# Token-row loads between the channel groups, and the third operand sum on VectorE before the second

## The chip, the cores and the metric

The kernel runs on one core of one Trainium2 chip. The metric is device time in microseconds of one execution; three runs of the kernel before are given by their median.

## The reference

A hybrid encoder layer is applied to two sequences (`x_prompt`, `x_sample`) of 1024 tokens by 1024 channels, in float32:

```
h = rmsnorm(x, norm_mix)
z = h @ w_in                      # 512 pooling, 3 x 768 attention (q, k, v)
a = pool_mixer(z[..., :512]) @ w_up_pool
b = attention_branch(z[..., 512:]) @ w_up_attn
g = sigmoid(h @ w_gate + b_gate)
x = x + (g_a * a + g_b * b) @ w_out
h = rmsnorm(x, norm_ffn)
x = x + (silu(h @ w_ffn_gate) * (h @ w_ffn_up)) @ w_ffn_down
y = rmsnorm(x, norm_final)
```

`rmsnorm` divides a token by the root of its mean square over the channels and multiplies by a gain per channel. The change touches only the first tens of microseconds: the first `rmsnorm` of the first sequence, the value columns of `h @ w_in` for two groups of heads, and the first pair of q and k columns.

## The kernel before, in words

**Precision.** Each float32 operand is split into a high part (a cast to fp32r, on ScalarE) and a low part (the rest, by a subtraction on GpSimd or VectorE). One product of two operands is three matmuls: high by high, high by low, low by high (`three`, lines 1334 to 1336).

**Products.** Most matrix products are done by a scheme with seven products instead of eight. The activations are cut into quarters: A11 and A12 are the first half of the tokens (half 0) with channels 0 to 511 and 512 to 1023, A21 and A22 those of half 1. Four sums are made of them: S1 = A21 + A22, S2 = S1 - A11, S3 = A11 - A21, S4 = A12 - S2. The products come in the order A11, S2, A12, S3, S1, A22, S4; each takes a weight operand (`t_hi`, `t_lo`) and 12 matmuls of 512 columns. The first pair of column blocks done so has the products 14 to 20; product 14 is A11, 15 is S2, 16 is A12, 17 is S3, 18 is S1.

**Opening.** Before these, the value columns of two head groups are computed directly (`direct_run`), with eight channel blocks k (128 channels each) of the transposed input, loaded as `xt` into `HT[h][p]` (half h, blocks 2p and 2p+1; a pair of blocks is called a channel group here). Run 0 takes token tiles 0 to 3 (half 0) unnormalised, four tiles by three matmuls per block; runs 1 and 2 take tiles 4, 5 and 6, 7 (half 1) normalised, six matmuls per block. The norm factors need the rows of `x` token by token (`x_rows[h][p]`, four loads per half): ScalarE squares and sums a row tile (`squares_of`), takes the root of four (`deviations`), VectorE inverts and spreads them (`factors`, tile `spread`), TensorE transposes the spread tile (`factor_rows`, put between the blocks of a direct run by the number given to it), and VectorE multiplies the channels by gain and factor (`channel_norms`). Half 1 is normalised first, then half 0. After that come casts (`open_his`, ScalarE), low parts (`open_low` on GpSimd, `open_lows` on VectorE) and sums (`open_sums` on GpSimd, `open_thirds` on VectorE).

**Order.** Every engine has its program written out by hand, in `opening` of its block; engines run their lists in order and wait on semaphores. SP issues the loads in the order of `first_tokens`, all on one queue. In the lists of ScalarE and GpSimd `operand_hi` and `leading_lows` make the high and low part of the weight operand of products 14 to 17; four more follow in the normal schedule. The buffers are placed by address: the high and low parts of S3 lie in `S` where half 1's channels lie, and the raw S2 has a buffer of its own, `s2_raw`; S3 is written over A11, S1 over A22, S4 over A12.

Of the kernel before, what the change touches and what calls it, by code (L numbers as in the profile page):

```python
# [13 lines left out]
P = 128  # L14
# [311 lines left out]
def encoder(nc, x, w_in, maps, w_up_pool, w_up_attn, w_gate, w_out, w_fg, w_fu, w_fd,  # L326
# [3 lines left out]
    with ctx:  # L330
# [35 lines left out]
        s2_raw = [at(f"s2_raw{i}", EX + 4096 * i, [2, H2]) for i in range(2)]  # L366
# [106 lines left out]
        ones_set, spread_ready, third_made, first_in, rows_in = (sem(n) for n in ("ones_set", "spread_ready", "third_made", "first_in", "rows_in"))  # L473
# [59 lines left out]
        def open_source(part, k):  # L533

            if part[0] == "A":
                ks = slice(k, k + 1)
                return channels(int(part[1] == "2"), part, ks), ks
            ks = slice(2 * k, 2 * k + 2)
            if part == "S1":
                return channels(1, "A22", ks), ks  # L540
            if part == "S2":
                return s2_raw[k][:, :, :].rearrange("q k (p c) -> q p k c", c=P), ks
            return channels(0, part, ks), ks
# [37 lines left out]
        def _(sp):  # L581
# [44 lines left out]
            def first_tokens():  # L626
# [9 lines left out]
                def rows(h, p):  # L636
                    sp.dma_start(x_rows[h][p][:, :], x_t[0, 4 * h + p]).then_inc(rows_in, 16)
# [4 lines left out]
                for p in range(4):  # L642
                    rows(1, p)
                for p in range(4):
                    sp.dma_start(HT[1][p][:, :, :], xt_k[:, 2 * p:2 * p + 2, H2:T]).then_inc(xh_in[p], 16)
                sp.wait_ge(ssx_ready, 4)
# [386 lines left out]
        def _(pool):  # L1033
# [200 lines left out]
            def open_sums(part, i):  # L1234
# [3 lines left out]
                if part == "S1":  # L1238
                    pool.wait_ge(xn_ready, XN_AT[1, 4 + 2 * i + 1])
                    for k in range(2 * i, 2 * i + 2):  # L1240
                        open_ready(pool, "A22", k)
                    out, a, b, op = s1, channels(1, "A21", ks), s1, ALU.add
                elif part == "S2":
                    pool.wait_ge(mix_made, SUMMED["S1", i])
                    out, a, b, op = s2, s1, channels(0, "A11", ks), ALU.subtract
                else:
                    pool.wait_ge(mix_made, SUMMED["S2", i])
                    for k in range(2 * i, 2 * i + 2):
                        open_ready(pool, "A12", k)
                    out, a, b, op = channels(0, "A12", ks), channels(0, "A12", ks), s2, ALU.subtract  # L1250
                nc.gpsimd.tensor_tensor(out, a, b, op).then_inc(mix_made, 1)

            def opening():
# [13 lines left out]
                leading_lows(0, 2, (0, 1))  # L1267
                for i in range(2):
                    open_sums("S4", i)
                leading_lows(0, 2, (2, 3))  # L1270
# [52 lines left out]
        def _(pe):  # L1323
# [265 lines left out]
            def warm_up():  # L1589
                pe.wait_ge(ones_set, 1)  # L1590
# [34 lines left out]
            def opening():  # L1625

                warm_up()
                direct_run(0, {5: 1})
                direct_run(1, {5: 0})
# [137 lines left out]
        def _(act):  # L1767
# [3 lines left out]
            act.wait_ge(eps_set, 1)  # L1771
# [315 lines left out]
            def squares_of(h, p):  # L2087

                act.wait_ge(rows_in, 64 if h else 128)
# [40 lines left out]
            def opening():  # L2130
# [5 lines left out]
                for p in range(4):  # L2136
                    squares_of(1, p)
                deviations(1)
# [171 lines left out]
        def _(dve):  # L2310
            nc.vector.memset(ones[:, :], 1.0).then_inc(ones_set, 1)
# [61 lines left out]
            def open_thirds():  # L2373

                for i in range(2):
                    ks = slice(2 * i, 2 * i + 2)
                    dve.wait_ge(mix_made, SUMMED["S2", i])
                    for k in range(2 * i, 2 * i + 2):
                        open_ready(dve, "A11", k)
                    a = channels(0, "A11", ks)  # L2380
                    V_.tensor_tensor(a, a, channels(1, "A21", ks), ALU.subtract).then_inc(third_made, 1)

            def opening():

# [589 lines left out]
```

## Time and profile before

| | us |
|---|---|
| three runs, median (lowest to highest) | 2507.11 (2505.29 to 2507.63) |
| the profiled execution, its own time | 2509.43 |
| its span in the profile | 2506.4 |
| TensorE busy in the span | 2477.3 (99%) |
| GpSimd busy | 1708.5 (68%) |
| VectorE busy | 1295.7 (52%) |
| ScalarE busy | 1030.9 (41%) |

The span is the time from the first to the last instruction that the profile shows; the execution's own time has some more around it. Busy shares are means over the whole span. Since TensorE is busy nearly throughout, its own pauses, and the stretches in which it is granted a lower clock, are what has to be read in detail; for the other engines the stretch around such a pause counts, not the share.

### The profile page before, as it was taken

To read this page: it belongs to the slowest core of one execution; us is meant where nothing else is said; L and a number is where in the kernel's file an instruction comes from. 1 tells how busy PE (TensorE), PEld (TensorE's weight loads), DVE (VectorE), ACT (ScalarE), POOL (GpSimd) and SP (SyncE) were. 2 spreads that over 40 slices of the span, in tenths; PEclk is the share of its full clock that TensorE was granted. 3 is DMA by queue.
4 is the path that set the end of the run, shared out by engine and by line. 5 is a ranking of instruction groups with operands and counts; after the bars stand their busy time and mean duration, and the time that the engine had idled before them with its cause. 6 is when DMAs were issued, how large, how long until landed. Compare 5 with 4: busy or idle time off the path is not lost. (4 is left out here: it accounts for less than half of the span.)

```text
span 2506.4 us, 33224 instructions
## 1 busy us (share of the span) xinstructions
PE 2477.3 (99%) x12032; PEld 2039.6 (81%) x12032; DVE 1295.7 (52%) x1740; ACT 1030.9 (41%) x1988; POOL 1708.5 (68%) x1258
## 2 busy tenths in 40 slices
PE   8999999999999999999999999999999999999998
PEld 6788877888888888888888888788888888888887
DVE  6774546645422222387956745456462222224768
ACT  6324553445433333346452245534453333333445
POOL 6865456545888888755687754573468888887544
PEclk9999999999999999999999999999999999999999
DMA  7345556462333333474353445656523332435543
GB/s 245 126 126 160 157 161 188 163 253 76 97 93 97 119 95 101 139 237 166 127 180 90 128 144 162 182 158 207 204 84 94 113 100 91 125 93 177 185 128 141
DMA packets 330272, 357.95 MB, mean 143 GB/s; under 512 B 39168, under 2 KB 234368, under 8 KB 328576
## 3 DMA queue, kind: packets, MB, share of 16 engines
q1 hardware_dynamic: 328528, 352.58, 44.2%
q10 hardware_dynamic: 1584, 3.26, 0.4%
q8 instruction: 97, 1.59, 0.3%
q14 instruction: 63, 0.52, 0.1%
HBM read 254.39 MB, written 101.38 MB: 142 GB/s over the span
## 5 line engine op out<-in xcount | busy, mean ns | idle before, releaser
L1334 PE MATMUL ps<-S,t_hi 128*128 128x512 f32 (+1 forms) x2264 | 890.3, 393 | 13.9 <-POOL t_lo L1084 11.9
L1336 PE MATMUL ps<-S,t_lo 128*128 128x512 f32 (+1 forms) x2264 | 879.7, 389 | 0.0
L1335 PE MATMUL ps<-S,t_hi 128*128 128x512 f32 (+1 forms) x2264 | 878.9, 388 | 0.0
L1334 PEld LDWEIGHTS ps<-S,t_hi 128*128 128x128 f32 x2264 | 426.1, 188 | 106.5 <-POOL t_lo L1084 14.4
L1336 PEld LDWEIGHTS ps<-S,t_lo 128*128 128x128 f32 x2264 | 425.9, 188 | 87.9
L1335 PEld LDWEIGHTS ps<-S,t_hi 128*128 128x128 f32 x2264 | 426.5, 188 | 84.7 <-issue 1.0
L1084 POOL TENSOR_TENSOR t_lo<-wraw,t_hi 128x512 fp32r<-128x512 f32 x175 | 237.3, 1357 | 186.7 <-ACT t_hi L1865 184.2
L1084 POOL TENSOR_TENSOR t_lo<-wraw_ff,t_hi 128x512 fp32r<-128x512 f32 x225 | 289.1, 1286 | 78.7 <-ACT t_hi L1865 68.6
L1084 POOL TENSOR_TENSOR t_lo<-R,t_hi 128x512 fp32r<-128x512 f32 x154 | 219.6, 1430 | 175.8 <-ACT t_hi L1865 175.6
L1865 ACT CAST t_hi<-wraw_ff 128x512 fp32r<-128x512 f32 x225 | 139.9, 623 | 364.5 <-PE ps L1336 363.2
L1334 PE MATMUL ps<-t_hi,d_hi 128*128 128x512 f32 x616 | 240.5, 390 | 0.0
L1336 PE MATMUL ps<-t_hi,d_lo 128*128 128x512 f32 x616 | 239.8, 389 | 0.0
L1335 PE MATMUL ps<-t_lo,d_hi 128*128 128x512 f32 x616 | 239.7, 389 | 0.0
L1865 ACT CAST t_hi<-wraw 128x512 fp32r<-128x512 f32 x175 | 109.2, 625 | 238.9 <-PE ps L1336 234.0
L2736 DVE TENSOR_TENSOR d_lo<-d_raw,d_hi 128x512 fp32r<-128x512 f32 x154 | 141.6, 921 | 95.8 <-ACT d_hi L2064 94.3
L2501 DVE TENSOR_TENSOR u<-u,ps 128x512 f32<-128x512 f32 x80 | 54.9, 687 | 259.3 <-PE ps L1336 259.2
L2064 ACT CAST d_hi<-d_raw 128x512 fp32r<-128x512 f32 x154 | 95.6, 621 | 173.9 <-PE ps L1336 160.7
L2504 DVE TENSOR_TENSOR v<-u,ps 128x512 f32<-128x512 f32 x80 | 55.0, 687 | 190.2 <-PE ps L1336 189.7
L1084 POOL TENSOR_TENSOR t_lo<-t,t_hi 128x512 fp32r<-128x512 f32 x70 | 94.2, 1346 | 84.5 <-ACT t_hi L1865 84.1
L1084 POOL TENSOR_TENSOR t_lo<-t_ff,t_hi 128x512 fp32r<-128x512 f32 x90 | 117.9, 1310 | 31.5 <-ACT t_hi L1865 31.5
L1216 POOL TENSOR_TENSOR wo_lo<-wo_raw,wo_hi 128x1024 fp32r<-128x1024 f32 x32 | 82.0, 2571 | 80.2 <-ACT wo_hi L2029 80.2
L1336 PEld LDWEIGHTS ps<-t_hi,d_lo 128*128 128x128 f32 x616 | 115.6, 188 | 24.4
(229 smaller groups left out, 4011.4 us busy)
## 6 DMA issues: line engine op xcount, KB each, us to landing
d_raw<-d_rows SPq DMA_DIRECT2D x154, 256.0 KB, 2.8
d_rows<-act_f SPq DMA_DIRECT2D x110, 256.0 KB, 2.2
wraw_ff<-w_ffn_up SPq DMA_DIRECT2D x44, 512.0 KB, 4.5
R<-w_ffn_down SPq DMA_DIRECT2D x88, 256.0 KB, 3.1
sp_rows<-gst SPq DMA_DIRECT2D x80, 256.0 KB, 2.2
wraw_ff<-w_ffn_gate SPq DMA_DIRECT2D x40, 512.0 KB, 5.0
wraw<-w_in SPq DMA_DIRECT2D x38, 512.0 KB, 6.0
wo_raw<-w_out SPq DMA_DIRECT2D x36, 512.0 KB, 3.7
```

Source lines behind the costliest of these rows:

```text
L1084: nc.gpsimd.tensor_tensor(shape(t_lo[r][:, :]), src, shape(t_hi[r][:, :]).bitcast(F32), ALU.subtract).then_inc(t_ready, 1)
L1216: nc.gpsimd.tensor_tensor(wo_lo[r][:, :], wo_raw[op % 3][:, :], wo_hi[r][:, :].bitcast(F32), ALU.subtract).then_inc(wo_ready, 1)
L1334: nc.tensor.matmul(o_ps, w[0], r[0], start=begins, stop=False, skip_group_check=True)
L1335: nc.tensor.matmul(o_ps, w[0], r[1], start=False, stop=False, skip_group_check=True)
L1336: return nc.tensor.matmul(o_ps, w[1], r[0], start=False, stop=ends, skip_group_check=True)
L1865: nc.scalar.copy(dst, src).then_inc(thi_ready, 1)
L2064: nc.scalar.copy(d_hi[d % 4][:, :], d_raw[d % 4][:, :]).then_inc(dhi_ready, 1)
L2501: V_.tensor_tensor(u, u, b1, ALU.add).then_inc(sums_done, 1)
L2504: V_.tensor_tensor(v1[:, :], u, b2, ALU.add).then_inc(sums_done, 1)
L2736: V_.tensor_tensor(d_lo[d % 4][:, :], d_raw[d % 4][:, :], d_hi[d % 4][:, :].bitcast(F32), ALU.subtract).then_inc(d_ready, 1)
```

## The change

**Loads.** SP issues two of half 1's four row loads behind channel group 1 and two behind group 2, ahead of groups 2 and 3; before, all four came behind group 3. ScalarE squares them between the casts of the groups, in two pairs that wait on two semaphores, and the root of half 1 comes ahead of the casts of group 3. SP releases half 0's row loads after two squares instead of four. VectorE makes half 1's factors after six of the eight raw splits. TensorE transposes half 1's factors behind block 4 of run 0 (before: block 5), and half 0's behind block 1 of run 1 (before: block 5).

**Sums.** VectorE forms S3 in a buffer of its own (where the raw S2 stood) right after the splits of A12, without waiting for S2; GpSimd writes S2 over A11 and waits for S3 first. On GpSimd the third low part of a weight operand comes ahead of the S4 sums.

```diff
-        s2_raw = [at(f"s2_raw{i}", EX + 4096 * i, [2, H2]) for i in range(2)]
+        s3_raw = [at(f"s3_raw{i}", EX + 4096 * i, [2, H2]) for i in range(2)]
...
+            if part == "S3":
+                return s3_raw[k][:, :, :].rearrange("q k (p c) -> q p k c", c=P), ks
             if part == "S2":
-                return s2_raw[k][:, :, :].rearrange("q k (p c) -> q p k c", c=P), ks
+                return channels(0, "A11", ks), ks
...
                 for p in range(4):
                     rows_of_first(p)
                     columns(p)
-                for p in range(4):
-                    rows(1, p)
+                    if p in (1, 2):
+                        rows(1, 2 * p - 2)
+                        rows(1, 2 * p - 1)
                 for p in range(4):
                     sp.dma_start(HT[1][p][:, :, :], xt_k[:, 2 * p:2 * p + 2, H2:T]).then_inc(xh_in[p], 16)
-                sp.wait_ge(ssx_ready, 4)
+                sp.wait_ge(ssx_ready, 2)
                 for p in range(4):
                     rows(0, p)
...
                 elif part == "S2":
                     pool.wait_ge(mix_made, SUMMED["S1", i])
+                    pool.wait_ge(third_made, i + 1)
+                    for k in range(2 * i, 2 * i + 2):
+                        open_ready(pool, "A11", k)
                     out, a, b, op = s2, s1, channels(0, "A11", ks), ALU.subtract
...
-                leading_lows(0, 2, (0, 1))
+                leading_lows(0, 2, (0, 1, 2))
                 for i in range(2):
                     open_sums("S4", i)
-                leading_lows(0, 2, (2, 3))
+                leading_lows(0, 2, (3,))
...
                 warm_up()
-                direct_run(0, {5: 1})
-                direct_run(1, {5: 0})
+                direct_run(0, {4: 1})
+                direct_run(1, {1: 0})
                 direct_run(2, {})
...
-                act.wait_ge(rows_in, 64 if h else 128)
+                act.wait_ge(late_rows_in if h and p > 1 else rows_in, 32 if h else 96)
...
                     elif part == "S3":
                         act.wait_ge(third_made, 2)
+                        act.wait_ge(mix_made, SUMMED["S2", 1])
...
                     raw_his(k)
-                for p in range(4):
-                    squares_of(1, p)
-                deviations(1)
+                    if k in (2, 4):
+                        squares_of(1, k - 2)
+                        squares_of(1, k - 1)
+                    if k == 4:
+                        deviations(1)
...
                     ks = slice(2 * i, 2 * i + 2)
-                    dve.wait_ge(mix_made, SUMMED["S2", i])
-                    for k in range(2 * i, 2 * i + 2):
-                        open_ready(dve, "A11", k)
-                    a = channels(0, "A11", ks)
-                    V_.tensor_tensor(a, a, channels(1, "A21", ks), ALU.subtract).then_inc(third_made, 1)
+                    a21, a11 = channels(1, "A21", ks), channels(0, "A11", ks)
+                    V_.tensor_tensor(open_source("S3", i)[0], a11, a21, ALU.subtract).then_inc(third_made, 1)
...
-                raw_lows(range(KD))
+                raw_lows(range(6))
                 factors(1)
+                raw_lows(range(6, KD))
...
-                open_lows(DVE_OPEN[8:12])
                 open_thirds()
-                open_lows(DVE_OPEN[12:])
+                open_lows(DVE_OPEN[8:])
```

The load queue of SP, from channel group 1 on, before. `ht_1_78` to `ht_3_80` are the channel groups 1 to 3 of half 0, `wraw_both` the weights that go with them, `x_rows_0_89` to `x_rows_3_92` half 1's rows:

```order
L629 DMA ht_1_78<-xt 128x2x512
L633 DMA wraw_both<-w_in 128x2x512
L629 DMA ht_2_79<-xt 128x2x512
L633 DMA wraw_both<-w_in 128x2x512
L629 DMA ht_3_80<-xt 128x2x512
L637 DMA x_rows_0_89<-x 128x1024
L637 DMA x_rows_1_90<-x 128x1024
L637 DMA x_rows_2_91<-x 128x1024
L637 DMA x_rows_3_92<-x 128x1024
```

The same place with the change:

```order
L632 DMA ht_1_78<-xt 128x2x512
L640 DMA x_rows_0_89<-x 128x1024
L640 DMA x_rows_1_90<-x 128x1024
L636 DMA wraw_both<-w_in 128x2x512
L632 DMA ht_2_79<-xt 128x2x512
L640 DMA x_rows_2_91<-x 128x1024
L640 DMA x_rows_3_92<-x 128x1024
L636 DMA wraw_both<-w_in 128x2x512
L632 DMA ht_3_80<-xt 128x2x512
```

The four row loads have moved up, two by two, ahead of groups 2 and 3; half 1's channel loads come behind these rows in both.

GpSimd from the S1 sums to the fourth weight operand, before. `ht_2_83` and `ht_3_84` become S1 there, `s_raw` is S2, `ht_2_79` and `ht_3_80` become S4; the `t_lo` rows are products 14 to 17 in order:

```order
L1251 TENSOR_TENSOR ht_2_83<-ht_0_81,ht_2_83 128x4x2x128 [waits mix_made,s_ready,xn_ready]
L1251 TENSOR_TENSOR ht_3_84<-ht_1_82,ht_3_84 128x4x2x128 [waits mix_made,s_ready,xn_ready]
L1251 TENSOR_TENSOR s_raw_116<-ht_2_83,ht_0_77 128x4x2x128 [waits mix_made]
L1251 TENSOR_TENSOR s_raw_117<-ht_3_84,ht_1_78 128x4x2x128 [waits mix_made]
L1084 TENSOR_TENSOR t_lo_137<-wraw_127,t_hi_132 128x512 [waits thi_ready]
L1084 TENSOR_TENSOR t_lo_136<-t_142,t_hi_131 128x512 [waits thi_ready]
L1251 TENSOR_TENSOR ht_2_79<-ht_2_79,s_raw_116 128x4x2x128 [waits s_ready,mix_made]
L1251 TENSOR_TENSOR ht_3_80<-ht_3_80,s_raw_117 128x4x2x128 [waits s_ready,mix_made]
L1084 TENSOR_TENSOR t_lo_138<-wraw_127,t_hi_133 128x512 [waits thi_ready]
L1084 TENSOR_TENSOR t_lo_139<-wraw_127,t_hi_134 128x512 [waits thi_ready,t_made]
```

The same place with the change, where `ht_0_77` and `ht_1_78` (A11) become S2:

```order
L1258 TENSOR_TENSOR ht_2_83<-ht_0_81,ht_2_83 128x4x2x128 [waits mix_made,s_ready,xn_ready]
L1258 TENSOR_TENSOR ht_3_84<-ht_1_82,ht_3_84 128x4x2x128 [waits mix_made,s_ready,xn_ready]
L1258 TENSOR_TENSOR ht_0_77<-ht_2_83,ht_0_77 128x4x2x128 [waits mix_made,third_made]
L1258 TENSOR_TENSOR ht_1_78<-ht_3_84,ht_1_78 128x4x2x128 [waits mix_made,third_made]
L1088 TENSOR_TENSOR t_lo_137<-wraw_127,t_hi_132 128x512 [waits thi_ready]
L1088 TENSOR_TENSOR t_lo_136<-t_142,t_hi_131 128x512 [waits thi_ready]
L1088 TENSOR_TENSOR t_lo_138<-wraw_127,t_hi_133 128x512 [waits thi_ready]
L1258 TENSOR_TENSOR ht_2_79<-ht_2_79,ht_0_77 128x4x2x128 [waits s_ready,mix_made]
L1258 TENSOR_TENSOR ht_3_80<-ht_3_80,ht_1_78 128x4x2x128 [waits s_ready,mix_made]
L1088 TENSOR_TENSOR t_lo_139<-wraw_127,t_hi_134 128x512 [waits thi_ready,t_made]
```

S2 has the new wait on `third_made`, and the `t_lo` of product 16 has moved from behind the S4 sums to ahead of them.

VectorE from the last A12 splits to the S4 splits, before. The rows with 128x4x256 are the low parts of S1 (`ht_2_83`, `ht_3_84`), S2 (`s_raw`), S3 (`ht_0_77`, `ht_1_78`) and S4 (`ht_2_79`, `ht_3_80`); the two with 128x4x2x128 are the S3 sums:

```order
L2370 TENSOR_TENSOR S<-ht_3_80,S 128x4x128 [waits shi_ready] x2
L2370 TENSOR_TENSOR S<-ht_2_83,S 128x4x256 [waits shi_ready]
L2370 TENSOR_TENSOR S<-ht_3_84,S 128x4x256 [waits shi_ready]
L2370 TENSOR_TENSOR S<-s_raw_116,S 128x4x256 [waits shi_ready]
L2370 TENSOR_TENSOR S<-s_raw_117,S 128x4x256 [waits shi_ready]
L2381 TENSOR_TENSOR ht_0_77<-ht_0_77,ht_0_81 128x4x2x128 [waits mix_made]
L2381 TENSOR_TENSOR ht_1_78<-ht_1_78,ht_1_82 128x4x2x128 [waits mix_made]
L2370 TENSOR_TENSOR S<-ht_0_77,S 128x4x256 [waits shi_ready]
L2370 TENSOR_TENSOR S<-ht_1_78,S 128x4x256 [waits shi_ready]
L2370 TENSOR_TENSOR S<-ht_2_79,S 128x4x256 [waits shi_ready]
L2370 TENSOR_TENSOR S<-ht_3_80,S 128x4x256 [waits shi_ready]
```

The same place with the change, where `s_raw` is S3 and `ht_0_77`, `ht_1_78` are S2:

```order
L2380 TENSOR_TENSOR S<-ht_3_80,S 128x4x128 [waits shi_ready] x2
L2388 TENSOR_TENSOR s_raw_116<-ht_0_77,ht_0_81 128x4x2x128
L2388 TENSOR_TENSOR s_raw_117<-ht_1_78,ht_1_82 128x4x2x128
L2380 TENSOR_TENSOR S<-ht_2_83,S 128x4x256 [waits shi_ready]
L2380 TENSOR_TENSOR S<-ht_3_84,S 128x4x256 [waits shi_ready]
L2380 TENSOR_TENSOR S<-ht_0_77,S 128x4x256 [waits shi_ready]
L2380 TENSOR_TENSOR S<-ht_1_78,S 128x4x256 [waits shi_ready]
L2380 TENSOR_TENSOR S<-s_raw_116,S 128x4x256 [waits shi_ready]
L2380 TENSOR_TENSOR S<-s_raw_117,S 128x4x256 [waits shi_ready]
L2380 TENSOR_TENSOR S<-ht_2_79,S 128x4x256 [waits shi_ready]
L2380 TENSOR_TENSOR S<-ht_3_80,S 128x4x256 [waits shi_ready]
```

The S3 sums have moved ahead of the S1 and S2 splits and have lost their wait.

## Rows read from the trace of the kernel before

**Rows 1.** The page, busy us, share of the span and instructions of each engine.
```profile
PE 2477.3 (99%) x12032; PEld 2039.6 (81%) x12032; DVE 1295.7 (52%) x1740; ACT 1030.9 (41%) x1988; POOL 1708.5 (68%) x1258
```

**Rows 2.** Waits of TensorE, 0 to 100 us: us in total, times, longest.
```profile
PE ps L1334 <- POOL t_lo L1084: 11.9, 2, 9.1
```

**Rows 3.** Stretches: length, busy us by engine, granted clock (PEclk), DMA share, GB/s.
```profile
59.40:69.70 10.30, 5.55 (x13) 4.39 (x14) 10.24 (x5) 3.34 (x6) 10.30 (x5) 0.50 0.16 52
76.50:79.90 3.40, 3.40 (x10) 2.62 (x9) 3.40 (x2) 0.18 (x1) 3.32 (x3) 0.50 0.00 0
79.90:95.00 15.10, 15.10 (x68) 12.49 (x67) 13.93 (x26) 4.56 (x8) 14.86 (x12) 1.00 0.45 140
```

**Rows 4.** Timeline of TensorE: start us, us, instruction, [idle before it <-releaser].
```profile
20.23 0.39 PE L1334 MATMUL ps<-extra_hi,raw_hi 128*128 128x512 f32 x1
...
40.80 0.63 PE L1599 MATMUL ps<-ident_sb,spread 128*128 128x128 f32 x4 [0.44 <-DVE spread L2341]
...
54.67 0.39 PE L1336 MATMUL ps<-extra_hi,S 128*128 128x512 f32 x1
...
64.15 0.79 PE L1334 MATMUL ps<-S,t_hi 128*128 128x512 f32 x1 [9.09 <-POOL t_lo L1084]
...
75.25 0.47 PE L1334 MATMUL ps<-S,t_hi 128*128 128x512 f32 x1 [2.79 <-POOL t_lo L1084]
...
82.43 0.39 PE L1334 MATMUL ps<-S,t_hi 128*128 128x512 f32 x1
```

**Rows 5.** Timeline of GpSimd from 40 us on.
```profile
43.76 5.96 POOL L1231 TENSOR_TENSOR S<-ht,S 128x512 fp32r<-128x512 f32 x4 [0.70 <-ACT S L2128]
...
55.27 6.61 POOL L1251 TENSOR_TENSOR s_raw<-ht,ht 128x1024 f32<-128x1024 f32 x2
61.85 2.25 POOL L1084 TENSOR_TENSOR t_lo<-wraw,t_hi 128x512 fp32r<-128x512 f32 x1
...
72.92 4.47 POOL L1084 TENSOR_TENSOR t_lo<-wraw,t_hi 128x512 fp32r<-128x512 f32 x2
...
79.69 2.16 POOL L1084 TENSOR_TENSOR t_lo<-t,t_hi 128x512 fp32r<-128x512 f32 x1
81.82 2.54 POOL L1084 TENSOR_TENSOR t_lo<-wraw,t_hi 128x512 fp32r<-128x512 f32 x2
```

**Rows 6.** Timeline of VectorE, 0 to 100 us.
```profile
7.79 12.34 DVE L2361 SCALAR_TENSOR_TENSOR raw_lo<-ht,gain_c,raw_hi 128x512 fp32r<-128x512 f32 x8 [6.79 <-ACT raw_hi L2084]
...
26.76 1.41 DVE L2351 SCALAR_TENSOR_TENSOR ht<-ht,gain_c,ps 128x512 f32<-128x512 f32 x2 [0.81 <-PE ps L1599]
...
41.47 4.04 DVE L2351 SCALAR_TENSOR_TENSOR ht<-ht,gain_c,ps 128x512 f32<-128x512 f32 x6 [0.81 <-PE ps L1599]
...
49.14 3.93 DVE L2370 TENSOR_TENSOR S<-ht,S 128x512 fp32r<-128x512 f32 x2
53.64 6.05 DVE L2370 TENSOR_TENSOR S<-ht,S 128x1024 fp32r<-128x1024 f32 x2 [0.57 <-ACT S L2128]
...
65.10 5.60 DVE L2381 TENSOR_TENSOR ht<-ht,ht 128x1024 f32<-128x1024 f32 x2
71.83 8.86 DVE L2370 TENSOR_TENSOR S<-ht,S 128x1024 fp32r<-128x1024 f32 x4 [1.12 <-ACT S L2128]
```

**Rows 7.** Timeline of ScalarE, 5 to 42 us.
```profile
15.37 1.34 ACT L2084 ACTIVATE raw_hi<-ht,gain_c 128x512 fp32r<-128x512 f32 x2 [0.29 <-DMA ht<-xt]
20.42 1.06 ACT L2090 ACTIVATE squares<-x_rows 128x1024 f32<-128x1024 f32 x1 [3.71 <-DMA x_rows<-x]
...
30.85 0.63 ACT L2128 CAST S<-ht 128x512 fp32r<-128x512 f32 x1 [0.64 <-DVE ht L2351]
32.94 1.06 ACT L2090 ACTIVATE squares<-x_rows 128x1024 f32<-128x1024 f32 x1 [1.46 <-DMA x_rows<-x]
```

**Rows 8.** Half 1's channel loads: issues (duration, first to last); the last, us to landing.
```profile
L645 SPq DMA_DIRECT2D ht<-xt x4: 570/1271/2329, 8.7 to 11.9; - x4
...
ht<-xt SPq DMA_DIRECT2D x1, 512.0 KB, 14.4
```

More of the change, by code:

```diff
@@ L472, in encoder @@
         upp_in = [sem(f"upp_in{r}") for r in range(2)]
-        ones_set, spread_ready, third_made, first_in, rows_in = (sem(n) for n in ("ones_set", "spread_ready", "third_made", "first_in", "rows_in"))
+        spread_ready, third_made, first_in, rows_in, late_rows_in = (sem(n) for n in (
+            "spread_ready", "third_made", "first_in", "rows_in", "late_rows_in"))
         sems = {name: sem(name) for name in PER_SEQ}
@@ L636, in rows @@
                 def rows(h, p):
-                    sp.dma_start(x_rows[h][p][:, :], x_t[0, 4 * h + p]).then_inc(rows_in, 16)
+                    sp.dma_start(x_rows[h][p][:, :], x_t[0, 4 * h + p]).then_inc(late_rows_in if h and p > 1 else rows_in, 16)
                 for p in range(4):
@@ L1589, in warm_up @@
             def warm_up():
-                pe.wait_ge(ones_set, 1)
+                pe.wait_ge(eps_set, 1)
                 for _ in range(WARM):
@@ L1770, in _ @@
                 act.dma_start(dst, src).then_inc(ident_in if src is ident else gmix_in if src is gmix else const_in, 16)
-            act.wait_ge(eps_set, 1)
+            act.wait_ge(eps_set, 2)
             nc.scalar.activation(root[:, :], eps[:, :], ACT.Sqrt)
@@ L2310, in _ @@
         def _(dve):
-            nc.vector.memset(ones[:, :], 1.0).then_inc(ones_set, 1)
+            nc.vector.memset(ones[:, :], 1.0).then_inc(eps_set, 1)
             nc.vector.memset(eps[:, :], EPS).then_inc(eps_set, 1)
```

## The prediction

> **What bounds the kernel now.** I read the page first: TensorE is busy 99% of a span of 2506.4 us [rows 1], so a change wins time only where TensorE stands still or runs slowly. The list of its waits over the first 100 us has one large entry: 11.9 us in two waits for the low halves `t_lo` that GpSimd makes [rows 2]. TensorE's timeline shows where: 9.09 us between the last direct matmul (54.67) and product 14 (64.15), and 2.79 us ahead of product 16 (75.25) [rows 4]. The stretches with their granted clock show what follows a wait: 59.4 to 69.7 and 76.5 to 79.9 ran at 0.50, which is 1.2 GHz, the rest at 2.4 GHz [rows 3]. At full clock a matmul takes 15.10/68 = 0.22 us of the engine, at half 5.55/13 = 0.43 [rows 3], 0.2 us more: 13 times 0.2 = 2.6 us behind the long wait, and half of a stretch of 3.4, 1.7 us, behind the short one. All that this opening could give back is 9.1 + 2.8 + 2.6 + 1.7 = 16 us.
>
> Who sets these waits? GpSimd has no gap worth naming from 43.76 on: A11 splits, S1 sums, S2 sums, `t_lo` of products 14 and 15, S4 sums, `t_lo` of 16 and 17, a weight sum, `t_lo` of 18 [rows 5]. Product 14 starts when its `t_lo` ends (61.85 + 2.25 = 64.10). Product 18 starts at 82.43 [rows 4] and its `t_lo` ended at 79.69 + 2.16 = 81.85 [rows 5], 0.58 us of slack. So **GpSimd's chain binds, and TensorE follows it with 0.58 us to spare**: in products 14 to 18 no more can be won than that slack plus what the chain is earlier at `t_lo` 18.
>
> The chain starts with the A11 casts, which wait for half 0's norm factors, which wait for half 0's token rows: ScalarE stood idle from the end of a cast (30.85 + 0.63) until the rows were in at 32.94, 1.46 us [rows 7].
>
> **The change part by part.**
> *Loads.* In a full queue one load of rows costs (20.42 - 15.37)/4 = 1.26 us, from the last channel group's casts to the squares that waited for the four loads behind it [rows 7]. Two rows ahead of channel group 2 make it 2.5 us later, four ahead of group 3 bring that to 15.37 + 5.05 = 20.4. Group 2 would then be in at about 15.2; its two casts take 1.34 [rows 7] and a VectorE split 12.34/8 = 1.54 [rows 6], so 18.1, and TensorE reaches channel 4 at 20.23 [rows 4]. Two microseconds cover it; group 3 is needed 5.4 us later and has the same cover. Without it the delay would still come out of the longer wait described next.
>
> The four rows of half 0 were issued when four squares were done, 20.42 + four times 1.06 = 24.7 [rows 7]. Now two squares release them, at about 14.7, and they stand directly behind half 1's channels. Those keep their place, since the bytes ahead of them are the same: the last is issued at 11.9 and lands 14.4 us later, at 26.3 [rows 8]. Four rows behind it: 26.3 + 5.05 = 31.4, against 32.94: 1.5 us earlier. The upper bound is ScalarE's own work ahead of them: group 3's four casts (1.34 for two) end by 20.4 + 2.7 = 23.1, and VectorE, which starts its two splits of 1.54 with the third cast, is through them at about 25.4, where half 1's norms began at 26.76 [rows 6]; 1.4 us earlier, the cast that stood ahead of the idle 1.46 ends at 30.1, so at most 2.8 us are won. The lower bound is nothing, if the queue gives the rows no better place. I take 1.5, the sum from rows: **everything from half 0's factors on moves 1.5 us forward**.
>
> *The factor transposes* move from behind channel 5 of the second direct run to behind channel 1, 24 matmuls earlier. TensorE was there at 40.80 - 0.44 [rows 4]; minus 24 times 0.22 it now arrives at 35.0. The factors come at 40.8 - 1.5 = 39.3. So **a new wait of 4.3 us appears in the direct runs**. Behind it queue the remaining direct matmuls; the norms on VectorE needed these transposes before too (0.81 us of wait at 41.47 [rows 6]). The direct runs end at 54.67 + 0.22 - 0.44 + 4.3 = 58.8.
>
> The clock makes that dearer. Behind both waits of before it was granted at 0.50 [rows 3], at a price of 1.7 and 2.6 us; a wait of 4.3 us lies between them, so the direct runs end at 60.5 to 61.4. The Trainium skill, TensorE: Matmul & The Clock Gate (What's actually happening), has the gate fall back to half rate when the engine has stood idle and open again only after sustained work; by that rule the new wait is not free, and both rows of 0.50 here agree. It costs nothing in the end while product 14's `t_lo` is later still, at 63.4 (below): 2 to 3 us of cover.
>
> *S3 early on VectorE.* It no longer waits for S2 and runs directly after the A12 splits, which ended at 49.14 + 3.93 = 53.07 [rows 6], now 51.6. Two S3 sums took 5.60, two S1 splits beside GpSimd's sums 6.05 [rows 6], so the first takes 2.8 to 3.3 and ends at 54.4 to 54.9. GpSimd came to S2 at 55.27 [rows 5], now 53.8. Since S2 now overwrites A11, it must wait for S3: 0.6 to 1.1 us, I take 0.85. All `t_lo` stand behind it: product 14's ends at 64.10 - 1.5 + 0.85 = 63.4. Part of this returns: VectorE's idle 0.57 and 1.12 us ahead of the S1 and S3 splits [rows 6] is used, so its opening work ends earlier, and GpSimd's `t_lo` beside a VectorE without such splits took 2.54/2 = 1.27 instead of 2.16 [rows 5]. I let it return the 0.85 by `t_lo` 18; the bounds are nothing and all of it.
>
> The Trainium skill, SBUF — State Buffer (Who interferes with whom), is sharper: a VectorE operation with two SBUF inputs and a GpSimd operation that reads SBUF take the shared port in turn, and the one that started first blocks the other. By it S3 would first wait out an S1 sum and then run alone, and S2 would be held for about as long; no row here shows the two apart, since both lengthen when paired.
>
> *Third operand ahead of S4.* `t_lo` 16 moves ahead of the S4 sums and is ready at 63.4 + 2.25 + 2.25 = 67.9, so product 16 no longer waits. But S4 and `t_lo` 17 behind it keep the same work ahead of them: 72.92 + 4.47 - 1.5 + 0.85 = 76.7 [rows 5]. **The 2.79 us stall goes to product 17.** TensorE there: product 15 needs the S2 splits, now behind S3 and S1 on VectorE: 51.6 + 5.60 + (65.10 - 53.64) = 68.7 [rows 6]. Products 15 and 16, 12 matmuls or 2.7 us each, end at 74.1, and product 17 waits 2.6 us, with half clock likely to follow as it did behind 2.79: 0 to 1.7 us of it before product 18.
>
> *Sum.* `t_lo` 18 ends at 81.85 - 1.5 = 80.35. Product 17 ends at 76.7 + 2.7 = 79.4, or 81.1 at half clock. Product 18 starts between 80.35 and 81.1, against 82.43: 1.3 to 2.1 us gained, taken as 1.7. From product 16 on TensorE did not wait in this stretch, and no edit touches what follows, so product 18's gain is the span's. The profiled execution took 2509.43 us (3.03 around its span), 2.3 above the median 2507.11 of three runs: 2509.43 - 1.7 = 2507.7, and 2505.4 for the median. With the bounds (rows 0 to 2.8 earlier, 0.85 returned or not, half clock in or out) the gain is 0 to 3.4 us.
>
> **The rivals.** 0.2%, about what a measurement of this kernel can tell from no change, is 5.0 us.
> *No gain:* the rows land no earlier, or S2's wait is not returned and the half clock falls into products 17 and 18. For it: the slack of 0.58 is less than the 0.85. Against: ScalarE's 1.46 us of idle ended with these very rows. Time 2507.1, up to 2508.
> *Clearly faster:* the rows are so early that the factors meet TensorE without a wait, 4.3 us more than the 1.7: 2501.1. They would have to be in by 27.1, and they stand behind a load that lands at 26.3.
> *Clearly slower:* the clock stays at 1.2 GHz from the new wait to the end of product 14. Then 36 + 48 direct matmuls cost 16.8 us more, the direct runs end at 75.6, product 14 at half clock at 80.7, product 18 starts at 88.9, 6.5 us late: 2513.6. It decides from the point where the direct runs end after 71.5, four products of 2.7 us ahead of 82.43. Against: behind 9.09 us of wait full clock was back within 5.6 us of the restart at 64.15 [rows 3, 4].
>
> **How the numbers follow.** The forecast, 0 to 3.4 us gained (2503.7 to 2507.1), 70%; no gain 20%; clearly faster 6%; clearly slower 4%. The first two lie within 0.2%: 90%. The range covers both of them, widened by 1.5 to 1.7 us, about what lies between the lowest of the three runs (2505.29) and the middle one: 2502.0 to 2508.6.
>
> **What would show it.** Right: squares of half 0 begin near 31.4; the transposes wait some 4.3 us for `spread`, with half clock behind; the wait before product 14 shrinks from 9.1 to 2 or 3; none before 16, about 2.6 before 17; GpSimd idles under 1.1 us before S2; product 18 at 80.4 to 81.1. Wrong: rows in at 33, or before 29; direct runs ending behind product 14's `t_lo`; S2 held for over 2 us; a new TensorE wait behind product 18.

## The result and the profile after

The changed kernel takes **2510.99 us** (median of 20 runs, 2509.74 to 2512.36), the kernel before 2507.61 (20 runs, 2505.29 to 2509.34): ratio 1.0014, 95% interval 1.0008 to 1.0020. It is about 3.4 us slower, within the 0.2% that the prediction called no change, but on the wrong side of it and outside the range of 2502.0 to 2508.6. The execution with a profile took 2510.32 us, with a span of 2508.3.

The page's busy line answers to [rows 1]; nothing in it explains 3 us:

```profile
PE 2479.3 (99%) x12032; PEld 2042.3 (81%) x12032; DVE 1289.7 (51%) x1740; ACT 1031.1 (41%) x1988; POOL 1706.0 (68%) x1258
```

TensorE's waits over the first 100 us, where [rows 2] had one line of 11.9 us for `t_lo`:

```profile
PE ps L1606 <- DVE spread L2351: 6.3, 1, 6.3
PE ps L1341 <- ACT u L1884: 5.4, 1, 5.4
PE ps L1341 <- POOL t_lo L1088: 2.9, 1, 2.9
```

The second line is new and was in no part of the prediction: TensorE waits for `u`, the copy of product 14's result that ScalarE makes. The timeline of TensorE shows where (transposes, last direct matmul, products 14 to 18; to be read beside [rows 4]):

```profile
40.38 0.87 PE L1606 MATMUL ps<-ident_sb,spread 128*128 128x128 f32 x3 [6.26 <-DVE spread L2351]
...
61.70 0.39 PE L1343 MATMUL ps<-extra_hi,S 128*128 128x512 f32 x1
...
64.97 0.64 PE L1341 MATMUL ps<-S,t_hi 128*128 128x512 f32 x1 [2.88 <-POOL t_lo L1088]
...
69.40 0.39 PE L1341 MATMUL ps<-S,t_hi 128*128 128x512 f32 x1
...
77.68 0.77 PE L1341 MATMUL ps<-S,t_hi 128*128 128x512 f32 x1 [5.40 <-ACT u L1884]
...
82.63 0.40 PE L1341 MATMUL ps<-S,t_hi 128*128 128x512 f32 x1
...
85.39 0.39 PE L1341 MATMUL ps<-S,t_hi 128*128 128x512 f32 x1
```

Product 14 starts 0.82 us later than before, product 15 at the old time (69.40 against 69.44), product 16 at 77.68 against 75.25, product 18 at 85.39 against 82.43. So the loss arises at product 16 (2.43 us) and grows to 2.96 by product 18, in a stretch at half clock of 6.8 us where before had 3.4 (below, and [rows 3]). That is most of the 3.4 of the medians.

ScalarE around that copy, in the changed kernel (the S4 casts, `u`, the next operand):

```profile
72.73 1.04 ACT L2136 CAST S<-ht 128x1024 fp32r<-128x1024 f32 x1 [5.05 <-POOL ht L1258]
76.01 1.05 ACT L2136 CAST S<-ht 128x1024 fp32r<-128x1024 f32 x1 [2.23 <-POOL ht L1258]
76.96 0.58 ACT L1884 COPY u<-ps 128x512 f32<-128x512 f32 x1
77.43 0.62 ACT L1872 CAST t_hi<-t 128x512 fp32r<-128x512 f32 x1
```

The copy needs only product 14, done when product 15 starts at 69.40, but stands behind the second S4 cast, which waits for GpSimd's S4 sum. Product 16 needs the copy because it adds its result into the bank, a slice of `ps`, in which product 14's result stands. In the kernel before, ScalarE in the same place, and GpSimd's `t_lo` of product 16:

```profile
70.74 3.89 ACT L2128 CAST S<-ht 128x1024 fp32r<-128x1024 f32 x4 [5.77 <-DVE ht L2381]
74.53 0.58 ACT L1877 COPY u<-ps 128x512 f32<-128x512 f32 x1
```
```profile
72.92 2.25 POOL L1084 TENSOR_TENSOR t_lo<-wraw,t_hi 128x512 fp32r<-128x512 f32 x1
```

The copy ended at 75.11 and `t_lo` at 75.17. Product 16 had waited for both, 0.06 us apart, and [rows 2] name the one that came last.

GpSimd in the changed kernel, beside [rows 5]: a weight sum, the S2 sums, `t_lo` of 14, 15 and 16, the S4 sums, `t_lo` of 17, and of 18.

```profile
38.43 1.26 POOL L1134 TENSOR_TENSOR t<-wraw,t 128x512 f32<-128x512 f32 x1
...
56.12 6.58 POOL L1258 TENSOR_TENSOR ht<-ht,ht 128x1024 f32<-128x1024 f32 x2 [1.21 <-issue]
62.67 2.25 POOL L1088 TENSOR_TENSOR t_lo<-wraw,t_hi 128x512 fp32r<-128x512 f32 x1
64.88 2.27 POOL L1088 TENSOR_TENSOR t_lo<-t,t_hi 128x512 fp32r<-128x512 f32 x1
67.10 2.27 POOL L1088 TENSOR_TENSOR t_lo<-wraw,t_hi 128x512 fp32r<-128x512 f32 x1
69.33 6.64 POOL L1258 TENSOR_TENSOR ht<-ht,ht 128x1024 f32<-128x1024 f32 x2
75.94 2.25 POOL L1088 TENSOR_TENSOR t_lo<-wraw,t_hi 128x512 fp32r<-128x512 f32 x1
...
80.49 1.27 POOL L1088 TENSOR_TENSOR t_lo<-t,t_hi 128x512 fp32r<-128x512 f32 x1
```

VectorE, beside [rows 6], from half 0's factors to S3 (here a group of two), and ScalarE's first squares of half 0 with their deviations, beside [rows 7]:

```profile
38.23 0.18 DVE L2350 RECIPROCAL rstdx<-stdx 128x4 f32<-128x4 f32 x1 [2.34 <-ACT stdx L2104]
38.44 1.79 DVE L2351 TENSOR_TENSOR spread<-ones,rstdx 128x512 f32<-128x512 f32 x1
41.51 0.75 DVE L2361 SCALAR_TENSOR_TENSOR ht<-ht,gain_c,ps 128x512 f32<-128x512 f32 x1 [1.27 <-PE ps L1606]
...
52.57 4.55 DVE L2388 TENSOR_TENSOR s_raw<-ht,ht 128x1024 f32<-128x1024 f32 x2
```
```profile
31.43 1.06 ACT L2097 ACTIVATE squares<-x_rows 128x1024 f32<-128x1024 f32 x1 [2.78 <-DMA x_rows<-x]
...
37.90 0.30 ACT L2104 ACTIVATE stdx<-ssx,eps 128x4 f32<-128x4 f32 x1
```

The stretches at half clock and the one behind them, in the columns of [rows 3]:

```profile
37.90:44.70 6.80, 4.32 (x13) 3.57 (x14) 5.16 (x7) 4.67 (x9) 4.75 (x5) 0.50 0.27 60
65.20:68.60 3.40, 3.40 (x9) 2.62 (x9) 3.40 (x3) 2.48 (x4) 3.40 (x2) 0.50 0.46 154
75.40:82.20 6.80, 4.52 (x11) 3.59 (x12) 4.44 (x3) 2.67 (x4) 6.72 (x5) 0.50 0.01 1
82.20:95.00 12.80, 12.80 (x58) 10.56 (x57) 9.86 (x18) 3.12 (x5) 11.46 (x10) 1.00 0.37 124
```

### The profile page after: what moved, and what is told of

Read it like the earlier page. It is cut to its first block and busy times, and to the rows that moved or that the text cites. A ratio compares the mean times of both kernels' runs of the same rounds, so it can differ in the third digit from the quotient of the medians.

```text
span 2508.3 us, 33226 instructions
## 1 busy us (share of the span) xinstructions
PE 2479.3 (99%) x12032; PEld 2042.3 (81%) x12032; DVE 1289.7 (51%) x1740; ACT 1031.1 (41%) x1988; POOL 1706.0 (68%) x1258
```

## The experiments

Eleven kernels, five rounds each; the medians of before were 2507.5 to 2507.9 in these batches. The starts of the products, and of ScalarE's first squares of half 0, are from one profile of each kernel. Product 21 is the first of the next group of seven weights; behind it the next two follow at 2.72 us each (results first needs 2.85 for one), so its distance to 90.59 is what the opening hands on. A part of it can be lost later: from 100 us on TensorE's waits sum to between 6.1 and 7.8 us in these profiles, 7.1 before and 6.3 in the changed kernel.

| kernel | squares | 14 | 16 | 17 | 18 | 21 | to before | ratio (95% interval) |
|---|---|---|---|---|---|---|---|---|
| before | 32.94 | 64.15 | 75.25 | 79.42 | 82.43 | 90.59 |  |  |
| changed | 31.43 | 64.97 | 77.68 | 82.63 | 85.39 | 93.55 | +2.96 | 1.0014 (1.0008, 1.0020) |
| copy early | 31.70 | 65.25 | 72.17 | 78.56 | 82.90 | 91.06 | +0.47 | 1.0002 (0.9993, 1.0011) |
| spread first | 31.55 | 63.99 | 76.70 | 81.11 | 83.86 | 92.02 | +1.43 | 1.0012 (1.0003, 1.0020) |
| both | 31.74 | 64.19 | 70.55 | 77.49 | 82.78 | 91.14 | +0.55 | 0.9998 (0.9989, 1.0007) |
| old order | 31.66 | 65.22 | 76.29 | 80.62 | 83.34 | 91.50 | +0.91 | 1.0007 (0.9999, 1.0016) |
| order alone | 32.22 | 63.44 | 76.17 | 81.43 | 84.28 | 92.44 | +1.85 | 1.0008 (0.9999, 1.0017) |
| loads alone | 31.81 | 64.21 | 75.36 | 80.61 | 83.50 | 91.66 | +1.07 | 1.0003 (0.9994, 1.0012) |
| S3 alone | 34.00 | 66.34 | 77.40 | 81.64 | 84.36 | 92.52 | +1.93 | 1.0000 (0.9991, 1.0009) |
| S3 and order | 32.36 | 64.70 | 77.43 | 82.57 | 85.31 | 93.47 | +2.88 | 1.0013 (1.0004, 1.0022) |
| lows, then S4 | 31.64 | 64.07 | 71.26 | 73.98 | 80.87 | 91.58 | +0.99 | 1.0005 (0.9996, 1.0013) |
| lows first | 31.67 | 64.09 | 71.00 | 73.72 | 76.44 | 93.29 | +2.70 | 1.0012 (1.0003, 1.0021) |
| results first | 31.96 | 64.39 | 72.61 | 75.33 | 78.05 | 87.74 | -2.85 | 0.9990 (0.9981, 0.9998) |

An interval spans some 2.2 us to either side, so kernels a microsecond apart are not told apart by time. The starts are finer, but they are of single executions, and not free of chance: half 0's squares wait for a load, and in the four kernels with the old loads, which their edits leave alone, they began anywhere from 32.22 (order alone) to 34.00 (S3 alone).

```profile
32.22 1.06 ACT L2090 ACTIVATE squares<-x_rows 128x1024 f32<-128x1024 f32 x1 [1.12 <-DMA x_rows<-x]
```
```profile
34.00 1.06 ACT L2096 ACTIVATE squares<-x_rows 128x1024 f32<-128x1024 f32 x1 [1.51 <-DMA x_rows<-x]
```

GpSimd's A11 splits follow the squares by 10.81 or 10.82 us in all four kernels with the old loads, so such a shift is handed on in full to GpSimd's chain, and comparisons among these four are best made from the squares on.

**Copy early.** The changed kernel, with ScalarE's copy between its S3 and S4 casts:

```diff
-                open_his(OPEN_HIS[20:])
+                open_his(OPEN_HIS[20:22])
+                first_product(0, 2)
+                open_his(OPEN_HIS[22:])
...
```

(The rest skips the copy where it stood.)

> The change, with one move on ScalarE: the copy u of product 14's result comes ahead of the S4 casts instead of behind them. Queue theory (product 16 adds into the bank that this copy reads, and the copy stands behind casts that wait for S4, which the third operand has pushed back): the 5.4 us wait of TensorE on u is gone, product 16 starts near 72.1 directly behind product 15, a wait of about 3 us for t_lo comes ahead of product 17 instead (78.2), product 18 starts at 81.8 to 82.6 against 85.39 with the change and 82.43 before; 2.8 to 3.6 us faster than the change, ratio to before about 0.9998. Clock theory (the half-rate stretches behind the new waits are what costs): product 18 stays within 1 us of 85.39, because the half-rate stretches stay. S2 theory (S2's wait for S3 is what costs): product 18 gains at most 1 us.

The wait for `u` is gone. TensorE at products 16, 17 and 18:

```profile
72.17 0.39 PE L1341 MATMUL ps<-S,t_hi 128*128 128x512 f32 x1
...
78.56 0.80 PE L1341 MATMUL ps<-S,t_hi 128*128 128x512 f32 x1 [3.52 <-POOL t_lo L1088]
...
82.90 0.39 PE L1341 MATMUL ps<-S,t_hi 128*128 128x512 f32 x1
```

This is the picture the prediction had drawn for the change itself: no wait at 16, the stall at 17. Moving one 0.58 us copy brings product 18 back by 2.49 us (2.8 to 3.6 expected) and the median to 2508.01. Both rivals had at most 1 us. The queue theory is shown; the half clock behind the new wait takes part of the gain.

**Spread first.** The changed kernel, with GpSimd's second weight sum held until VectorE has spread the factors:

```diff
                 first_pair_sum(0, 2)
+                pool.wait_ge(spread_ready, 2)
                 second_pair_sum(0, 2)
```

> The change, with GpSimd's second weight sum waiting until half 0's spread tile is made. Port theory (the spread took 1.79 instead of 0.69 us because GpSimd's sum had started 0.01 us ahead of it, both reading two inputs from SBUF): the spread takes 0.69 again, is ready at 39.1 instead of 40.24, TensorE's wait for it falls from 6.3 to 5.2, half 0's norms start at 40.4 instead of 41.5, GpSimd's A11 splits at 42.2 instead of 43.3, product 18 about 1.1 us earlier than 85.39; ratio to before 1.0009 to 1.0011. Rival (the spread was slowed by something else, say the stretch itself): it stays at 1.8 and nothing moves, or it becomes short and nothing behind it moves since the weight sums now end 1.1 us later.

VectorE, then GpSimd, at that place:

```profile
38.57 0.69 DVE L2352 TENSOR_TENSOR spread<-ones,rstdx 128x512 f32<-128x512 f32 x1
40.54 0.75 DVE L2362 SCALAR_TENSOR_TENSOR ht<-ht,gain_c,ps 128x512 f32<-128x512 f32 x1 [1.27 <-PE ps L1607]
```
```profile
39.34 1.28 POOL L1134 TENSOR_TENSOR t<-wraw,t 128x512 f32<-128x512 f32 x1 [0.86 <-DVE spread L2352]
```

The spread takes 0.69 instead of 1.79 us, and the norms start 0.97 us earlier than in the changed kernel. Over all thirteen profiles GpSimd's A11 splits follow the squares by 11.91 us in the four kernels whose spread takes 1.79 us, and by 10.81 or 10.82 in the other nine: the blocked spread costs the chain 1.10 us. Product 16 starts 0.98 us earlier, though it still waits 4.20 us for the copy, and product 18 1.53. In the time this is not resolved (2510.51, ratio 1.0012).

**Both.**

> Both of the other two edits together. Queue and port theories: they add, product 18 at 80.7 to 81.5, 4 us earlier than with the change and 1 to 1.7 earlier than before; ratio to before 0.9993 to 0.9996. Clock theory: within 1 us of the change. If the port edit does not reach product 18, it is as with the early copy alone, 81.8 to 82.6.

Product 16 starts at 70.55 and product 17, after 4.06 us of wait for its `t_lo` behind the S4 sums, at 77.49, 1.07 us earlier than with the copy alone. But the half-clock stretch around it is 6.9 us (76.30 to 83.20) instead of 3.5 (78.30 to 81.80), so product 18 is at 82.78 instead of 80.7 to 81.5: the longer stretch takes the lead back. This expectation missed.

**Old order.** The changed kernel with the third `t_lo` behind S4 again:

```diff
-                leading_lows(0, 2, (0, 1, 2))
+                leading_lows(0, 2, (0, 1))
                 for i in range(2):
                     open_sums("S4", i)
-                leading_lows(0, 2, (3,))
+                leading_lows(0, 2, (2, 3))
```

> The change, with the order on GpSimd put back: S4 ahead of the third operand; loads and S3 stay as changed. Queue theory: S4 comes 2.25 us earlier, ends at 73.7, the copy u ends at 75.3, t_lo of product 16 at 75.9, product 16 starts at 76.0 instead of 77.7 (before 75.25), product 18 at 82.9 to 83.7; 1.7 to 2.5 us faster than the change, ratio to before 1.0002 to 1.0006. S2 theory (only S2's wait for S3 counts): as with the change but for nothing, product 16 behind 77, ratio near 1.0014.

Product 18 starts at 83.34, product 21 2.05 us earlier than in the changed kernel; by the ratios half of the loss is gone.

**Order alone.** The kernel before with the opposite edit.

> The kernel before with one edit: t_lo 16 is made ahead of the two S4 sums, loads and S3 as before. Queue theory (product 16 waits for ScalarE's copy of product 14, which stands behind the S4 casts): t_lo 16 ready near 72.9 us, but the S4 sums end 2.25 us later, the copy moves from 74.53 to about 76.5, product 16 starts near 77.1 instead of 75.25 on a wait for that copy, product 18 near 84.5; the time is 1.7 to 2.5 us over before, ratio 1.0007 to 1.0010. Rival (t_lo 16 is the only thing that product 16 waits for, as the prediction had it): product 16 at 72.9, product 18 at 80.4 to 82.4, ratio 0.9992 to 1.0000. Second rival (the loss comes from the loads or from S3's new place): no change, 1.0000 with the copy at 74.5.

`t_lo` 16 ends at 65.57 + 2.26 = 67.83, five microseconds ahead of the expectation's 72.9, and product 16 starts later than before all the same, on the copy. Its start and the next `t_lo`:

```profile
76.17 0.77 PE L1334 MATMUL ps<-S,t_hi 128*128 128x512 f32 x1 [4.88 <-ACT u L1877]
```
```profile
65.57 2.26 POOL L1084 TENSOR_TENSOR t_lo<-wraw,t_hi 128x512 fp32r<-128x512 f32 x1
```

An operand made 7.3 us earlier loses 1.85 us at product 18, 2.57 measured from the squares, which began 0.72 us earlier here (about 2.1 expected): the queue theory again, in the kernel before.

**Loads alone.** The kernel before with the changed loads, squares and transposes.

> The kernel before with the loads' part of the change alone: rows of half 1 between the channel groups, squares, deviations and transposes in their new places; S3 and the order of the t_lo as before. Port theory: half 0's squares still start near 31.4, VectorE's spread for half 0 starts near 38.4 beside GpSimd's second weight sum and takes 1.79 instead of 0.69 us, half 0's A11 splits end about 0.4 us earlier than before (43.76 to about 43.3), product 14 starts near 63.7, product 16 near 74.8 to 75.3; ratio 0.9998 to 1.0000. Rival of the prediction (the whole 1.5 us arrives): A11 splits at 42.3, product 16 near 73.7, ratio 0.9994. Rival that the loads make the loss: product 18 1.5 us or more later than 82.43, ratio 1.0008 or more.

```profile
38.83 1.79 DVE L2345 TENSOR_TENSOR spread<-ones,rstdx 128x512 f32<-128x512 f32 x1
```
```profile
64.21 0.50 PE L1336 MATMUL ps<-S,t_hi 128*128 128x512 f32 x1 [0.97 <-POOL t_lo L1086]
...
75.36 0.76 PE L1336 MATMUL ps<-S,t_hi 128*128 128x512 f32 x1 [5.39 <-POOL t_lo L1086]
```
```profile
59.40:74.00 14.60, 9.60 (x41) 7.26 (x40) 13.17 (x6) 6.75 (x10) 14.60 (x6) 1.00 0.11 36
74.00:80.90 6.90, 5.54 (x13) 4.41 (x14) 6.90 (x5) 2.40 (x5) 6.82 (x4) 0.51 0.00 0
```
```profile
36.50:46.70 10.20, 5.94 (x16) 4.89 (x17) 6.75 (x9) 7.84 (x15) 8.15 (x7) 0.50 0.38 98
```

The spread is blocked as in the changed kernel. My expectation missed what the clock does. Around the wait for the transposes TensorE ran at half clock for 10.2 us here and for 6.8 in the changed kernel, so the direct runs end later and only 0.97 us of wait is left ahead of product 14. Without a long wait there the products 14 and 15 run at full clock, so TensorE reaches product 16 sooner, waits 5.39 instead of 2.79 us there, and pays a 6.9 us stretch at half clock where before paid 3.4. Product 18 is 1.07 us later although GpSimd's chain is not: its `t_lo` 18 ends at 79.75 + 2.16 = 81.91, against 81.85.

**S3 alone, and S3 with the order.** The kernel before with S3's part of the change, and the changed kernel with the loads of before.

> The kernel before with S3 made early in its own place and S2 in A11's place, loads and the order of the t_lo as before. Queue theory: GpSimd waits 1.0 to 1.5 us for S3 ahead of its S2 sums, t_lo 14 ends near 65.2, and the S4 sums, casts and the copy of product 14 follow about 1 us later, product 16 near 76.3, product 18 near 83.3; ratio 1.0003 to 1.0007. Rival (S3's place is free, the order of the t_lo alone loses): 1.0000 with product 18 at 82.4.

> The changed kernel with the loads, squares and transposes of before: S3 early and t_lo 16 ahead of S4, no more. Queue theory: as in the changed kernel product 16 waits for the copy of product 14 behind the S4 casts, and all of it stands 0.4 us later: product 16 near 78.1, product 18 near 85.8, ratio 1.0013 to 1.0016. Rival (the loads make the loss): product 18 near 83, ratio 1.0003 or less.

With S3 alone GpSimd waits 1.22 us ahead of S2 and product 18 is 1.93 us later, but 1.06 of that was there before the edit came into play, in the squares at 34.00. Measured from the squares it is 0.87, the 0.9 expected; the time (2508.21, ratio 1.0000) agrees with a small loss. S3 and order cost 3.46 from the squares (2.88 against the start of the span), where 3.4 was expected.

So from the squares on these parts add up: 2.57 for the order and 0.87 for S3 make 3.44, against 3.46 for both (at product 16, 1.64 and 1.09 against 2.76). The whole change costs 0.5 less than both (2.96), about the 0.42 by which the new loads bring the A11 splits forward. Loads alone cost 1.07 all the same, by the clock; what the loads are worth depends on where the half-clock stretches fall.

**Lows, then S4, and lows first.** Both rest on the kernel with both mends. The first makes all of `t_lo` 14 to 17 ahead of S4, the second `t_lo` 18 and its rounded operand too (the line with 18 is in the second only):

```diff
-                leading_lows(0, 2, (0, 1, 2))
+                leading_lows(0, 2, (0, 1, 2, 3))
+                low_part(0, 18, t_of(0, 2)[0][:, :, :])
                 for i in range(2):
                     open_sums("S4", i)
-                leading_lows(0, 2, (3,))
```

> The changed kernel with the early copy and the spread first, and all four t_lo 14 to 17 ahead of the S4 sums. Queue theory: the 4.06 us wait ahead of product 17 goes, since t_lo 17 ends near 70.9; product 17 at about 74.0, the S4 sums at 70.9 to 76.4, the fourth weight sum to 77.7, t_lo 18 to 79.0, product 18 at about 79.0 instead of 82.78; no stretch at half clock after 70 us, since no wait over 2 us is left. Time about 3 to 3.8 us under copy_and_spread, ratio to before 0.9984 to 0.9987. Rival (the products after the opening are bound by something later, so that a lead here is lost): product 18 at 79.0 but the ratio 0.9995 to 1.0000. Second rival (the clock falls all the same): product 18 at 82 or later, ratio 0.9998 or more.

> As lows_then_s4, with t_lo 18 and its rounded operand ahead of the S4 sums as well. Queue theory: product 17 at about 74.0, product 18 at 77.5 with no wait, the S4 sums at 72.5 to 77.5, the fourth weight sum to 78.8, t_lo 19 to 81 or 82, product 19 at 81 to 82 with a wait of up to 1 us, product 20 at about 85 where before had 89.2; time 3.5 to 4.3 us under before, ratio 0.9983 to 0.9987. Rival (bound later): product 20 at 85 but the ratio 0.9995 to 1.0000. Second rival (the S4 operands are late now, their casts standing behind sums that end at 77.5): a wait of 2 us or more ahead of product 20, ratio 0.9990 or more.

Both expectations missed: ratios of 0.9983 to 0.9987 were forecast, 1.0005 and 1.0012 measured. Products 17 and 18 come when expected, or a microsecond sooner, where nothing else binds (73.98; 73.72 and 76.44), but each time the next product stalls: product 18 waits 4.01 us for its `t_lo`, which stands behind the fourth weight sum and S4; then product 19 waits for `v`, a sum that VectorE makes of earlier results, behind its S4 splits. Lows first, TensorE at product 19, and VectorE:

```profile
84.98 0.77 PE L1342 MATMUL ps<-S,t_hi 128*128 128x512 f32 x1 [5.66 <-DVE v L2515]
```
```profile
76.44 4.54 DVE L2384 TENSOR_TENSOR S<-ht,S 128x1024 fp32r<-128x1024 f32 x2 [4.61 <-ACT S L2137]
...
84.16 0.68 DVE L2515 TENSOR_TENSOR v<-u,ps 128x512 f32<-128x512 f32 x1
```

VectorE waited 4.61 us for the S4 casts and split for 4.54 us more, while products 15 and 17, from whose results `u` and `v` are made, had ended when products 16 and 18 started, at 71.00 and 76.44. Neither rival of these expectations had named this wait: it is the copy's mistake on another engine.

**Results first.** So every step that a product before product 20 needs goes ahead of S4, on all three engines (the rest of the edit holds the weight sum as in spread first and skips these steps where they stood):

```diff
-                leading_lows(0, 2, (0, 1, 2))
+                leading_lows(0, 2, (0, 1, 2, 3))
+                fourth_pair_sum(0, 2)
+                t1, b21 = t_of(0, 2)[0][:, :, :], quarters_of(0, 2)[2]
+                low_part(0, 18, t1)
+                low_part(0, 19, b21)
                 for i in range(2):
                     open_sums("S4", i)
-                leading_lows(0, 2, (3,))
+                low_part(0, 20, quarters_of(0, 2)[3])
...
+                first_product(0, 2)
+                for m in (18, 19, 20):
+                    operand_hi(0, m)
+                open_his(OPEN_HIS[22:])
...
                         after_product(s, m - 1)
+                    if s == 0 and m in (18, 19):
+                        open_lows([("S4", m - 18)])
```

> The changed kernel with the early copy and the spread first, all of t_lo 14 to 19 and the fourth weight sum ahead of the S4 sums, the rounded operands 18 to 20 ahead of ScalarE's S4 casts, and VectorE's sums of the products 15 and 17 ahead of its S4 splits: whatever a product before product 20 needs stands ahead of S4 in every list. Queue theory (each of the waits seen so far was a small step queued behind S4's parts): products 16 to 19 follow one another at 2.72 us from about 71.0 to 79.2 without a wait, S4's splits end near 82, product 20 starts at 82 to 83 where the kernel before has 87.87, product 21 at 85 to 87 where before has 90.59; time 3.5 to 5.5 us under before, ratio 0.9978 to 0.9986. Rival (the clock gives it back): a half-clock stretch of 6.8 us behind the one wait of about 3 us ahead of product 14 or 20, product 21 at 88 to 90, ratio 0.9990 to 1.0000. Second rival (a lead at product 21 is lost to a later bound): product 21 at 87 or earlier but the ratio 0.9995 or more.

```profile
PE ps L1346 <- POOL t_lo L1088: 4.1, 2, 3.5
PE ps L1346 <- DVE S L2389: 0.5, 1, 0.5
```
```profile
63.20:70.00 6.80, 5.61 (x13) 4.45 (x14) 6.80 (x5) 3.99 (x8) 6.80 (x4) 0.50 0.23 77
70.00:95.00 25.00, 23.88 (x104) 19.11 (x104) 20.58 (x29) 8.38 (x13) 24.69 (x16) 1.00 0.38 111
```

These are TensorE's waits from 62 to 100 us (one of 3.5 ahead of product 14, then none over 0.6) and its stretches: full clock from 70 on. The median is 2505.26 (2504.61 to 2506.70) against 2507.85, 0.10% faster than before, and by the two ratios 0.24% faster than the changed kernel. It is less than expected (3.5 to 5.5 us), and the expectation's first rival, the clock, had named most of what is missing: the half clock ran 6.8 us around product 14's start, so product 16 came at 72.61 instead of 71.0. Products 16 to 19 then followed at 2.72 us, as expected. Product 20 waited 0.54 us for the second S4 split and product 21 0.59 for its `t_lo`; product 21 came at 87.74, between the 85 to 87 expected and the rival's 88 to 90.

## Why the prediction was wrong

**The step that failed** is "so product 16 no longer waits". I read the wait of 2.79 us ahead of product 16 as a wait for `t_lo` alone. The product adds to product 14's bank and also needs ScalarE's copy of it, and that copy stands behind the S4 casts. By moving `t_lo` 16 ahead of the S4 sums the change makes that operand ready at 69.37 instead of 75.17, and puts its 2.27 us ahead of the S4 sums, which with S2's wait end at 75.97 instead of 72.96; the copy behind them ends at 77.54 instead of 75.11. Order alone and copy early show it from both sides. Of the 2.96 us at product 18, these runs put 2.57 on the order and 0.87 on S3, less some 0.5 for the loads, by difference. The prediction followed the moved instruction through GpSimd's queue and not the chain from what was pushed back, S4, through the casts into `u`.

**A term mis-sized:** "everything from half 0's factors on moves 1.5 us forward". Squares at 31.43 (31.4 predicted) and `stdx` at 37.90, 1.52 us earlier than before, are right, the closeness in part by luck: the nine profiles with the new loads have the squares at 31.43 to 31.96, the four with the old at 32.22 to 34.00. Then GpSimd's weight sum started 0.01 us ahead of the spread; the spread took 1.79 us and ended at 40.23, against 40.65 before: 0.42 is left. GpSimd's A11 splits start that much earlier, at 43.34 against 43.76. For VectorE the transposes at half clock (37.9 to 44.7) used it up: the norms start at 41.51 against 41.47. Spread first shows the cause of the lost 1.1. I had checked the port for S3 alone, not for what the earlier factors would now meet.

**Right, or nearly.** The wait at the transposes was 6.26 us instead of 4.3, since the factors came 0.9 later and TensorE 0.9 earlier than worked out; the half clock came with it, 6.8 us of it, which agrees with what the prediction cited from the Trainium skill, TensorE: Matmul & The Clock Gate (What's actually happening), that the gate falls back to half rate when the engine has stood idle; and the direct runs ended at 61.70 + 0.39 = 62.1 (60.5 to 61.4 predicted) and stayed hidden behind `t_lo` 14, as predicted (2.88 us left of the 9.09). S2 waited 1.21 us for S3 (0.85 taken, 0.6 to 1.1 given): the profile labels it "issue", but the first S3 sum ended at 52.57 + 3.42 = 55.99 and S2 started at 56.12. It was returned by `t_lo` 18, which ended at 81.76 instead of 81.85: 0.82 late at `t_lo` 14, 0.09 early at 18. The 1.27 us row had carried that.

**What did not matter:** GpSimd's chain, in my words the one that binds, ended `t_lo` 18 earlier than before. TensorE reached product 18 3.6 us after it, where it had 0.58 us of slack before. The chain that binds had become another.

## What to carry to other kernels

The label on a wait names the semaphore that came last, so before an edit pulls that one forward, list every semaphore the instruction waits on and find when each was set; here the second came 0.06 us before the first. When work is moved ahead of other work on one engine, follow what was pushed back through every in-order queue that consumes it, and ask which small results (a copy, a sum) stand behind those consumers. A version that paid off moved all such small steps ahead of the late bulk work together; moving one at a time only moved the stall to the next product. And when profiles of single executions are compared, find a landmark ahead of the edit first: a load that landed 1.06 us late made more than half of what S3 alone seemed to cost.

## What the runs showed of the hardware

*A hundredth of a microsecond decides.* GpSimd's sum at 38.43 and the spread at 38.44: the spread takes 1.79 us (loads alone too, 38.81 and 38.83). Before, the spread at 39.96 and the sum at 40.00: the spread takes 0.69 and the sum 1.79. The later one pays. The Trainium skill, SBUF — State Buffer (Who interferes with whom), calls the port pair that VectorE and GpSimd share an exclusive lock, says that two-input VectorE operations contend with GpSimd's reads, and that issue order decides who blocks; these rows agree. The prediction held of the S3 sums that no row told first from second; the kernel before had such rows in the spread and the weight sum. S3 shows the same: 4.55 us for two, 3.42 for the one that began during an S1 sum, and 1.22 for the one at 55.91, which began 0.21 us ahead of GpSimd's S2 sum.

*The tail at half clock does not follow from the wait alone.* Its stretches were 3.4 to 3.5 us, or 6.8 to 6.9, or 10.2 to 10.3 (before; loads alone, at the transposes); waits of 3.5 went with either of the shorter two (3.5 in copy early, product 17; 6.8 in results first, product 14). So a shortened wait ahead of product 14 does not always save its tail, and in loads alone the clock that product 14 gained came back as a longer wait and a longer tail at product 16. What picks the length is left open here.
